# Token neighbours in a two-layer mixer: two transfers within SBUF for the neighbour matrix products

## The reference

```
def centred_shift(p):
    prev = jnp.pad(p[:, :-1], ((0, 0), (1, 0), (0, 0)))
    nxt = jnp.pad(p[:, 1:], ((0, 0), (0, 1), (0, 0)))
    return 0.5 * (prev + nxt)
...
    p = p + mu * (centred_shift(p) - p)
    r, k, v, dw, da, dg = jnp.split(p, RWKV_SPLITS, axis=-1)
```

## Time and profile before

| what | value |
|---|---|
| device time, median of 3 runs | 3302.87 us (3298.94 to 3304.57) |
| span of the profiled execution | 3296.8 us |
| TensorE busy | 2878.7 us, 87% |
| weight loads | 2021.6 us, 61% |
| VectorE busy | 2174.4 us, 66% |
| ScalarE busy | 1283.4 us, 39% |
| GpSimd busy | 580.6 us, 18% |
| moved by the DMA engines | 858.34 MB, mean 260 GB/s |

### The profile page before, as it was taken

The page is one execution under the profiler, slowest core; times in us unless marked ns, Lnnn a source line. Parts: engine busy times, 40 slices in busy tenths (PEclk is TensorE's granted clock), DMA queues, the critical chain, the costliest instruction groups (busy, mean ns, idle before and its releaser), DMA issues. The chain is left out here.

```text
span 3296.8 us, 49616 instructions
## 1 busy us (share of the span) xinstructions
PE 2878.7 (87%) x18746; PEld 2021.6 (61%) x18746; DVE 2174.4 (66%) x4086; ACT 1283.4 (39%) x2893; POOL 580.6 (18%) x516
## 2 busy tenths in 40 slices
PE   7999988799999998879988999997777799777777
PEld 7977787689897868858965765432322465222222
DVE  6665765586676566566664567777776577777774
ACT  4333432343433343154323424444444344444443
POOL 0000000000000000000000025444444054444442
PEclk9999999899999999999996999999999999999999
DMA  8565201376766530026564179999999699999997
GB/s 276 200 228 171 80 3 41 121 249 227 245 227 239 178 111 3 36 82 224 198 256 167 68 267 421 427 427 427 427 427 427 254 409 427 427 427 427 426 427 311
DMA packets 252569, 858.34 MB, mean 260 GB/s; under 512 B 15031, under 2 KB 138807, under 8 KB 179517
## 3 DMA queue, kind: packets, MB, share of 16 engines
q0 software_dynamic: 73728, 536.90, 38.7%
q1 hardware_dynamic: 178622, 318.59, 27.6%
HBM read 847.05 MB, written 8.39 MB: 259 GB/s over the span
## 5 line engine op out<-in xcount | busy, mean ns | idle before, releaser
L2987 POOL DMA_INDIRECT raw_weights<-peer_rows,expert_ids x208 | 234.0, 1125 | 2282.0 <-DVE expert_ids L148 2007.6
L778 DVE TENSOR_TENSOR weight_parts_lo<-raw_weights,weight_parts_hi 128x2048 fp32r<-128x2048 f32 (+7 forms) x173 | 387.0, 2263 | 147.3 <-ACT weight_parts_hi L747 147.3
L3097 PE MATMUL banks<-raw_weights,diagonals 128*128 128x512 f32 x832 | 399.2, 622 | 84.1 <-ACT diagonals L181 83.5
L747 ACT CAST weight_parts_hi<-raw_weights 128x2048 fp32r<-128x2048 f32 (+7 forms) x173 | 319.7, 1883 | 247.2 <-PE banks L449 203.2
L447 PE MATMUL banks<-normedT_hi,weight_parts_hi 128*128 128x256 f32 x1408 | 400.1, 284 | 14.5 <-DVE normedT_lo L153 9.3
L449 PE MATMUL banks<-normedT_hi,weight_parts_lo 128*128 128x256 f32 x1408 | 398.4, 283 | 0.0
L448 PE MATMUL banks<-normedT_lo,weight_parts_hi 128*128 128x256 f32 x1408 | 398.3, 283 | 0.0
L3097 PE MATMUL banks<-query_weights,diagonals 128*128 128x512 f32 x704 | 336.1, 617 | 63.7 <-ACT diagonals L181 63.3
L3097 PEld LDWEIGHTS banks<-raw_weights,diagonals 128*128 128x128 f32 x832 | 154.6, 196 | 319.5 <-ACT diagonals L181 170.3
L157 DVE CUSTOM_DVE_ANT_0 modulation<-raw_weights,normed 128x1024 f32<-128x1024 f32 x208 | 255.1, 1226 | 128.5 <-DMA raw_weights<-peer_rows,expert_ids 117.6
L3097 PE MATMUL banks<-modulation,diagonals 128*128 128x512 f32 x512 | 247.2, 619 | 62.5 <-ACT diagonals L181 62.2
(11 more groups left out here) (398 smaller groups left out, 5283.0 us busy)
## 6 DMA issues: line engine op xcount, KB each, us to landing
raw_weights<-ffn_in SPq DMA_DIRECT2D x88, 1024.0 KB, 7.5
side_weights<-mod_tiles SPq DMA_DIRECT2D x48, 1024.0 KB, 5.5
raw_weights<-ffn_out SPq DMA_DIRECT2D x44, 1024.0 KB, 7.0
raw_weights<-w_in SPq DMA_DIRECT2D x28, 1024.0 KB, 5.0
query_weights<-peer_w_q SPq DMA_DIRECT2D x16, 1024.0 KB, 10.7
raw_weights<-w_in SPq DMA_DIRECT2D x10, 1536.0 KB, 6.6
raw_weights<-w_branch SPq DMA_DIRECT2D x8, 1024.0 KB, 7.3
raw_weights<-w_out SPq DMA_DIRECT2D x8, 1024.0 KB, 6.7
```

The lines of the kernel that those rows point to most:

```text
L747: nc.scalar.copy(parts.hi[:, u, cs], raw[:, cs]).then_inc(high, 1)
L778: nc.vector.tensor_tensor(parts.lo[:, u, cs], raw[:, cs], parts.hi[:, u, cs].bitcast(F32), ALU.subtract).then_inc(low, 1)
L2987: nc.gpsimd.indirect_dma_start(out=ring.rows(g), out_offset=None, in_=table, in_offset=bass.IndirectOffsetOnAxis(ap=ids[:, n, t:t + 1], ax ...
L3097: last = nc.tensor.matmul(k.bank(2 * j + half), diag[:, g % DIAGS, :], ring.rows(g)[:, D + half * BANK:D + (half + 1) * BANK], start=t == ...
```

## The change

The constant matrix, `shift`, `differ` and the semaphore `delta` go. In their place:

- SP first issues four transfers. Three copy each token's predecessor from `p` to `delta`: partitions 0 to 111 to partitions 1 to 112, partitions 112 to 126 to 113 to 127, both for the two token blocks at once, and partition 127 of block 0 to partition 0 of block 1. The fourth puts a row of zeros, from HBM, where the first token's predecessor would be. The mixing factors, the parameters and tile 2 are issued behind them.
- GpSimd waits for these four and issues three transfers in the other direction, with the addition done by the transfer: each token's successor is added to what lies in `delta`.
- VectorE waits for the three (semaphore `neighbours`) ahead of the mix. The mix has one more operation, a fused 0.5 x delta - p. Its column groups are now the last 384 and the first 1,536.
- Split 3 comes behind the mix of the 384 columns, and split 4 between the two wide mixes. `take(0)` comes ahead of cast 3.
- TensorE runs half 0 to half 3 without anything between them.

```
-    s = np.arange(SEQ)
-    neighbour = 0.5 * (np.abs(s[:, None] - s[None, :]) == 1)
-    parts["shift"] = neighbour.reshape(NT, P, NT, P).transpose(1, 0, 2, 3)
...
+    whole, split_at = slice(0, C_RWKV), P // 16 * 16 - 16
+    before = [(slice(1, split_at + 1), slice(0, NT), slice(0, split_at), slice(0, NT)),
+              (slice(split_at + 1, P), slice(0, NT), slice(split_at, P - 1), slice(0, NT)),
+              (slice(0, 1), slice(1, NT), slice(P - 1, P), slice(0, NT - 1))]
+    after = [(from_, js, to, js_from) for to, js_from, from_, js in before]
+    no_token = nc.inline_tensor(np.zeros((1, C_RWKV), np.float32), name=f"no_token_{k.names}").ap()
...
             @block.sync
             def _(sp):
+                for to, js, from_, js_from in before:
+                    sp.dma_start(delta[to, js, :], p[from_, js_from, whole]).then_inc(S["part_in0"], 16)
+                sp.dma_start(delta[0:1, 0, :], no_token).then_inc(S["part_in0"], 16)
                 sp.dma_start(mur, rows(mu)).then_inc(S["loaded"], 16)
...
+            @block.gpsimd
+            def _(pool):
+
+                pool.wait_ge(S["part_in0"], 16 * (len(before) + 1))
+                for to, js, from_, js_from in after:
+                    nc.gpsimd.dma_start(delta[to, js, :], p[from_, js_from, whole],
+                                        accum_op=ALU.add).then_inc(k.neighbours, 16)
...
-                shift(0)
-                half(0)
-                half(1)
-                shift(1)
-                half(2)
-                half(3)
+                for i in range(4):
+                    half(i)
                 pe.wait_ge(S["lows_made"], 3)
-                pe.wait_ge(S["delta"], 8)
...
-                for i in range(4):
+                for i in range(3):
                     cast(i)
                 take(0)
+                cast(3)
...
                 def mix(j, cs):
+                    o.stt(delta[:, j, cs], delta[:, j, cs], 0.5, p[:, j, cs], ALU.mult, ALU.subtract)
                     o.mul(delta[:, j, cs], delta[:, j, cs], mur[:, cs])
                     return o.add(p[:, j, cs], p[:, j, cs], delta[:, j, cs])
...
                 split(0)
-                differ(0)
                 split(1)
                 split(2)
-                split(3)
-                differ(1)
+                dve.wait_ge(k.neighbours, k.shifts + 16 * len(after))
                 dve.wait_ge(S["loaded"], 16)
                 for j in range(NT):
-                    mix(j, slice(3 * cw, C_RWKV)).then_inc(S["lows_mixed"], 1)
-                split(4)
+                    mix(j, slice(3 * DA, C_RWKV)).then_inc(S["lows_mixed"], 1)
+                split(3)
                 for j in range(NT):
-                    mix(j, slice(0, 3 * cw))
+                    mix(j, slice(0, 3 * DA))
+                    if j == 0:
+                        split(4)
                 split(5)
```

More of the change, by code:

```diff
@@ L213, in __init__ @@
         self.fills = [0] * 6
+        self.neighbours, self.shifts = ctx.enter_context(nc.semaphore("neighbours")), 0
         self.preloaded = False
@@ L989, in prepare @@
     size = KC // 2 * BANK
-    cw = C_RWKV // 4
     l0 = 3 * DA
@@ L993, in prepare @@
     base = [f * 1 for f in k.fills]
-    order = (3, 0, 1, 2)
+    whole, split_at = slice(0, C_RWKV), P // 16 * 16 - 16
[4 more added lines that the diff above has]
+    no_token = nc.inline_tensor(np.zeros((1, C_RWKV), np.float32), name=f"no_token_{k.names}").ap()
     with ExitStack() as c:
@@ L1040, in half @@
                     last.then_inc(S["used"], 1)
[L1042 to L1049, removed]
                 def lora(what):
@@ L1233, in prepare @@
             k.fills[i % 2] += 16
+        k.shifts += 16 * len(after)
         k.preloaded = False
@@ L3127 @@
 SEMAPHORES = (["loaded", "turned", "copied_v", "copied_s", "squared", "rooted", "reduced", "summed", "drained",
-               "used", "pre_done", "biased", "squashed", "shifted", "delta", "lows_mixed", "lows_made", "lows_turned", "lows_copied", "lora_made",
+               "used", "pre_done", "biased", "squashed", "shifted", "lows_mixed", "lows_made", "lows_turned", "lows_copied", "lora_made",
                "kk_summed", "kd_made", "exped", "masked", "prod", "got",
```

## The result

| | before | after |
|---|---|---|
| device time, median of 4 runs | 3303.67 us (3298.94 to 3304.57) | 3329.01 us (3325.77 to 3334.78) |
| span of the profiled execution | 3296.8 us | 3332.7 us |
| tile 2's cast behind the stage's start, layers 1 and 2 | 16.3, 17.9 | 37.1, 37.2 |
| end of `half(5)` behind the stage's start, layers 1 and 2 | 53.6, 53.0 | 68.6, 68.8 |

What follows compares the result with a forecast made beforehand. Bound in one stage per layer by TensorE, then by tile 2's late landing in a full DMA queue. Layer 1 +6.9, layer 2 +9.0, smaller table -0.6: +15.3 on 3302.9 gives 3318 us, range 3298 to 3341.

Steps and rivals of the forecast that it cites:

- rival 3: Accumulating transfers are slow, worth four copies (19.2 us): +38.5 us in all, 3341 us; chance 22%.
- Removed, 12.2 us of TensorE per layer, of which 3.2 usable: Neighbour products free 12.2 us per layer, but the weight tile lets `half(2)` start at most 3.2 us sooner.
- rival 2: The copies cost nothing either, tile 2 stays at 16.35 and the saved pause remains: -9.5 us, 3293 us; chance 8%.
- The copies, 4.8 us; landing at 7.2: SP's added transfers move 1.97 MB at 409 GB/s ahead of tile 2, 4.8 us, landing 7.2 after stage start.
- The accumulation, 7.6 us: GpSimd's adding transfers delay tile 2 by two copies, 9.6 us, less 2 for a hole in the traffic: 7.6.
- Tile 2's landing, 28.8: The weight tile for `half(2)` lands 28.8 us after layer 1's stage start in place of 16.35: 16.35 + 4.8 + 7.6.
- Landing + 31.7: `half(5)` ends 31.7 us behind tile 2's landing: 4.2 cast and split, 21.7 VectorE's chain, 5.8 `half(5)`.
- The general form, 2 x (copies + accumulation) - 9.5: Whole kernel's added time from per-layer transfer costs; breaks even at 4.75 us of added engine time per layer.
- The accumulation's own landing is covered, by 29.8 at the latest: Added neighbours land by about 29.8 even at half share; VectorE needs them only at 33.0, so the wait costs nothing.
- The idle TensorE, 13 to 33, and its clock: TensorE idles from about 13 to 33 after stage start, clock 0.50 behind it, hidden by VectorE's chain.
- rival 1: The accumulation costs nothing, fitting into holes in the traffic; only 4.8 us added per layer, 3303 us; chance 12%.
- rival 4: The accumulation costs one copy's worth, 4.8 us: +9.7 us in all, 3313 us; chance 15%.

Runs made afterwards that it cites:

- b4: The changed kernel with all seven neighbour transfers left out, other work and orders kept: 3288.69 us, 0.9965 of the kernel before.
- a1: The changed kernel without the accumulating transfers, copies kept: 3308.49 us, 1.0015 of the kernel before.
- c1: The changed kernel with only the shifted 112-partition transfer each way, small pieces and row of zeros left out: 3315.93 us, 1.0062 of the kernel before.
- a3: The changed kernel with one unshifted 128-partition transfer each way in place of three, no row of zeros: 3321.81 us, 1.0055 of the kernel before.
- a2: The changed kernel with GpSimd's three transfers copying in place of adding: 3323.27 us, 1.0065 of the kernel before.
- c2: The changed kernel with small pieces and row of zeros issued ahead of the large piece in each direction: 3332.34 us, 1.0112 of the kernel before.
- d1: The changed kernel with only 112-partition transfers, plus two small copies of 15 neighbouring partitions in front of SP's queue: 3318.98 us, 1.0079 of before.
- d2: The changed kernel with only 112-partition transfers, plus two small copies of 15 partitions lying 8 apart: 3318.24 us, 1.0072 of the kernel before.
- a4: The changed kernel with weight tiles 2 and 3 issued ahead of the ten parameter loads: 3312.18 us, 1.0036 of the kernel before.
- b3: The changed kernel with SP's order alone changed: tiles 2 and 3 behind the copies, then mixing factors, parameters behind tile 4: 3313.53 us, 1.0043 of before.

## Why the prediction was right, and by how much not

The direction and the mechanism were right: the removed products freed TensorE for a wait on tile 2, and the new transfers made tile 2 later by more than was saved. Both transfers were sized too small, and the sum, 3318, is 11 us short of 3329; the range held the result because it reached to rival 3.

- *Removed, 12.2 us of TensorE per layer, of which 3.2 usable.* Nearly: in b4 `half(2)` starts at 19.7, 4.1 sooner, as its tile 2 landed 0.9 sooner. `half(0)` starts at 276.02 - 274.62 = 1.4. b4 shows the bound: 11.6 us for both layers where rival 2 had 9.5.
- *The copies, 4.8 us; landing at 7.2.* Too small. a1 gives 7.9 on tile 2 (6.1 in layer 2), and they landed at 12.0. 409 GB/s was the rate of loads from HBM; the copies ran at 265 to 288 with full engines, and their small pieces and the row of zeros held them until 12.0 (9.3 in c1 without these). SP's issue of the four took 5.8 us and not 1.8; that the backlog covers it is likely from c1 and not shown apart.
- *The accumulation, 7.6 us.* Too small: 12.9 (a1), 10.8 of it the engines' own time. The working had two halves, twice a copy and less 2 for a hole. The factor is 1.4 and not 2, but on a copy of 7.6 us and not 4.8; and the hole gave nothing: a share of 1.14 at 185 GB/s was not free time, and GpSimd was released at 12.0, behind the place of the hole (9 to 11).
- *Tile 2's landing, 28.8.* 37.1: 16.3 + 7.9 + 12.9. This is the step that failed, by 8.3 us, 3.1 from the copies and 5.3 from the accumulation. Against the same bytes in one transfer each way (a3), 5.6 us are the price of the cut into pieces, for which the prediction had no term at all.
- *Landing + 31.7.* Right to 0.1 us, in the change and in eight further runs (a1, a2, a3, b4, c1, c2, d1, d2: 31.6 in each, layer 1). The general form, 2 x (copies + accumulation) - 9.5, gives 2 x 20.8 - 9.5 = 32.1 with the measured sizes; the stages show 30.9, the medians 25.3 [22 to 31]; what makes up the rest between these two is open. The 9.5 was 5.5 for layer 1, 3.4 for layer 2 and 0.6 for the table; b4's ends, 47.0 and 47.8, give 6.6 and 5.2 for the layers.
- *The accumulation's own landing is covered, by 29.8 at the latest.* Covered, yes, but later than said: in the change the last of the three landed 18.5 us behind its issue, at about 32. a4 and b3, which take tile 2 out of the way, found it at 32.0 and 32.4, and there it decided. "Half share" was wrong too: from 292 to 300 its packets took 93% of the engines' time.
- *The idle TensorE, 13 to 33, and its clock.* The halves 0 and 1 end at 289.03, 14.4 after the start, and the pause is 26.95 us. The granted clock was at 0.50, the 1.2 GHz level, in the stretches from 296 on and still from 318 to 320, in and behind this pause; as predicted it hid behind VectorE's chain.
- *Rivals.* Rivals 1, 2 and 4 are refuted by a1, which finds 7.9 and 12.9 us where they had 4.8 at most for each. Copies and accumulation together: the forecast had 12.4 us per layer, rival 3 had 24.0, measured are 20.8. By its landing the case was nearer to rival 3; the median, 3329, lies between 3318 and 3341.

## What to carry to other kernels

Before moving work from a busy engine to transfers, look at the moment it is moved to: here the queue was full, so the transfers' engine time came out of the next weight tile, and the three other orders of issue gave back only about half of the loss (1.0036 to 1.0043 in place of 1.0081). A second queue is no way around a full one: packets of 7,680 bytes with an addition alternated with packets of 2,048 bytes, and the loads fell to 45 GB/s. Price a transfer in the time of the engines and not in bytes at the best rate seen: here a copy within SBUF took 1.4 to 1.6 times as long as a load, 1.4 times that again with an addition, and cutting off pieces of 15 partitions and of one came on top. And first ask what the removed work really blocks: of 24.4 us of products only some 11.6 could be had, and moving two splits, with the products kept, got 5.3 [1.7 to 8.6] without any transfer.

## What the runs showed that was not expected

- Engines with a share of 0.96 to 1.08 moved 409 GB/s from HBM, 260 to 288 within SBUF, and 222 to 230 where an accumulation and loads share them.
- 1.96 MB take 10.8 us of all 16 engines when they are added (9.5 as one transfer), 7.6 when they are copied.
- Two busy queues started equally many packets (195 and 192 in 8 us), not equally many bytes (1.50 and 0.36 MB).
- The three accumulating transfers landed long after their issue beside a full SP queue, in the same run from 288 to 304 (count, KB, us from issue to landing):

```profile
raw_weights<-projected POOLq DMA_DIRECT2D x1, 225.0 KB, 16.5
raw_weights<-projected POOLq DMA_DIRECT2D x1, 7.5 KB, 18.5
```

  A row of 7.5 KB needed 18.5 us, as the last of three; issued first, in c2, it needed 5.6.
- Pieces of 15 partitions cost the tile behind them some 10 us per MB, on single profiles, and their own packets 4 to 6; the cause of the difference stays open.
- In the stage's first stretches the clock differs between kernels whose TensorE does the same there. All twelve kernels without the neighbour products have a pause of TensorE of 2.28 or 2.29 us at the start of layer 1's stage. Four of them (the change, a1, b4, c2) show a granted clock of 0.50 in a stretch of 2 us just behind it, the other eight stay at 1.00 in theirs. What decides between them is not shown.
